# Low parts over the raw chunk, seven raw and four high-part buffers, one instruction per expert chunk and engine

## The reference, cut to what matters

```python
for l in range(2):                     # two hybrid layers: attention, convolution, spatial gate, block attention
    x = x + hybrid_layer(x, ...)       # h @ w_in [1024, 3488], then y @ w_out [1024, 1024]
h = rmsnorm(x);  x = x + hybrid_mixer(h, ...)         # w_in [1024, 2048], w_out [1024, 1024]
h = rmsnorm(x);  x = x + (silu(h @ wg) * (h @ wu)) @ wd    # dense, 2816 wide
h = rmsnorm(x);  x = x + hybrid_mixer(h, ...)
h = rmsnorm(x);  x = x + moe(h)                       # 8 experts, 3584 wide, each token goes to 2
return rmsnorm(x)
```

```python
top_v, top_i = lax.top_k(h @ w_router, 2)
gates = softmax(top_v)                                # spread over the 8 experts as gate
y = sum(gate[:, e:e+1] * ((silu(h @ wg[e]) * (h @ wu[e])) @ wd[e]) for e in range(8))
```

## Time and profile before

| | us |
|---|---|
| runs, median (lowest to highest) | 1587.7 (1586.84 to 1590.16) |
| span of the profiled execution | 1585.3 |
| TensorE busy | 1519.5 (96%) |
| VectorE busy | 1293.3 (82%) |
| ScalarE busy | 1091.0 (69%) |
| GpSimd busy | 119.5 (8%) |
| DMA, moved | 462.70 MB, mean 292 GB/s |

### The profile page before, as it was taken

One profiled execution on the slowest core, in us unless ns is written; L12 is line 12 of the kernel. 1 busy time (PEld: TensorE's weight loads), 2 busy tenths in 40 slices (PEclk: granted clock), 3 DMA queues, 4 the chain that ended last, 5 costly groups with the idle time before them and its releaser, 6 DMA issues.

```text
span 1585.3 us, 20833 instructions
## 1 busy us (share of the span) xinstructions
PE 1519.5 (96%) x7379; PEld 1259.7 (79%) x7379; DVE 1293.3 (82%) x1595; ACT 1091.0 (69%) x1435; POOL 119.5 (8%) x242
## 2 busy tenths in 40 slices
PE   7999999999999999699999999999899999999995
PEld 5788788888888888588887788888788787788784
DVE  5686585566545556789999999999999999999998
ACT  3664565655434364278888788888788878788876
POOL 3433431101000010100000000000000000000000
PEclk9999999999999999699999999999999999999998
DMA  9645444535546554299999999999999999999995
GB/s 329 208 150 177 158 151 140 186 107 186 173 146 208 191 182 138 67 323 377 391 397 407 386 369 387 386 407 407 383 386 387 391 409 400 382 386 387 398 409 221
DMA packets 203364, 462.70 MB, mean 292 GB/s; under 512 B 7934, under 2 KB 12428, under 8 KB 203132
## 3 DMA queue, kind: packets, MB, share of 16 engines
q1 hardware_dynamic: 200304, 453.80, 78.5%
q0 software_dynamic: 1904, 5.38, 1.3%
q10 hardware_dynamic: 1052, 2.19, 0.4%
HBM read 460.29 MB, written 1.05 MB: 291 GB/s over the span
## 4 chain that ended last, share of the span: by engine, by line
PE 76%; DVE 10%; DMA 7%; issue 2%; DVEq 2%; ACT 2%; SPq 0%; ACTq 0%
PE ps L2080 8%; PE ps L2082 8%; PE ps L2081 8%; PE ps L2536 8%; PE ps L2538 7%; PE ps L2537 7%; PE ps L2551 7%; PE ps L2552 7%; DVE wlo_sb L1304 5%; DMA raw_sb<-moe_wu 4%; PE ps L2589 2%; DMA raw_sb<-w_in 2%; ACT whi_sb L929 1%; DMA raw_sb<-moe_wd 1%; PE ps L2498 1%
## 5 line engine op out<-in xcount | busy, mean ns | idle before, releaser
L1304 DVE TENSOR_TENSOR wlo_sb<-raw_sb,whi_sb 128x1024 fp32r<-128x1024 f32 x672 | 783.6, 1218 | 38.1 <-ACT whi_sb L929 35.8
L929 ACT ACTIVATE whi_sb<-raw_sb 128x1024 fp32r<-128x1024 f32 x672 | 667.2, 1051 | 156.5 <-PE ps L2538 102.5
L1296 DVE TENSOR_TENSOR wlo_sb<-raw_sb,whi_sb 128x1024 fp32r<-128x1024 f32 (+2 forms) x198 | 230.2, 1204 | 143.3 <-ACT whi_sb L921 142.3
L921 ACT ACTIVATE whi_sb<-raw_sb 128x1024 fp32r<-128x1024 f32 (+2 forms) x198 | 192.3, 1023 | 161.5 <-PE ps L2082 131.1
L2080 PE MATMUL ps<-whi_sb,xlo_sb 128*128 128x512 f32 (+2 forms) x544 | 213.2, 392 | 4.2 <-DVE xlo_sb L1343 4.2
L2081 PE MATMUL ps<-wlo_sb,xhi_sb 128*128 128x512 f32 (+2 forms) x544 | 209.0, 384 | 0.0
L2082 PE MATMUL ps<-whi_sb,xhi_sb 128*128 128x512 f32 (+2 forms) x544 | 208.9, 384 | 0.0
L2536 PE MATMUL ps<-whi_sb,xlo_sb 128*128 128x512 f32 x448 | 181.3, 405 | 4.5 <-DVE wlo_sb L1304 3.8
L2538 PE MATMUL ps<-whi_sb,xhi_sb 128*128 128x512 f32 x448 | 175.4, 391 | 0.0
L2551 PE MATMUL ps<-whi_sb,xhi_sb 128*128 128x512 f32 x448 | 175.2, 391 | 0.0
L2552 PE MATMUL ps<-wlo_sb,xhi_sb 128*128 128x512 f32 x448 | 174.6, 390 | 0.0
(11 more groups left out here) (386 smaller groups left out, 2107.3 us busy)
## 6 DMA issues: line engine op xcount, KB each, us to landing
raw_sb<-moe_wg SPq DMA_DIRECT2D x115, 1024.0 KB, 9.7
raw_sb<-moe_wu SPq DMA_DIRECT2D x112, 1024.0 KB, 10.2
raw_sb<-moe_wd SPq DMA_DIRECT2D x112, 1024.0 KB, 10.8
raw_sb<-w_in SPq DMA_DIRECT2D x40, 1024.0 KB, 5.2
raw_sb<-w_out SPq DMA_DIRECT2D x16, 1024.0 KB, 5.0
raw_sb<-ffn_wg SPq DMA_DIRECT2D x10, 1024.0 KB, 5.1
raw_sb<-ffn_wu SPq DMA_DIRECT2D x10, 1024.0 KB, 5.1
raw_sb<-ffn_wd SPq DMA_DIRECT2D x10, 1024.0 KB, 5.1
```

Source lines behind the costliest of these rows:

```text
L921: nc.scalar.activation(whi[i % SPLIT][:, c:c + k // 2, 0:n], raw[i % RAW][:, c:c + k // 2, 0:n], ACT.Copy).then_inc(hi_ready, 1)
L929: nc.scalar.activation(whi[i % SPLIT][:, c:c + KC // 2, :], raw[i % RAW][:, c:c + KC // 2, :], ACT.Copy).then_inc(hi_ready, 1)
L1296: op = V.tensor_tensor(wlo[i % SPLIT][:, c:c + k // 2, 0:n], raw[i % RAW][:, c:c + k // 2, 0:n], whi[i % SPLIT][:, c:c + k // 2, 0:n], ALU ...
L1304: op = V.tensor_tensor(wlo[i % SPLIT][:, c:c + KC // 2, :], raw[i % RAW][:, c:c + KC // 2, :], whi[i % SPLIT][:, c:c + KC // 2, :], ALU.su ...
```

## The change

Three things change at once.

1. The low part of a chunk is written over its own raw buffer, so there are as many low-part buffers as raw ones and no others. The raw buffers go from six to seven, the high-part buffers from three to four; in all 11 buffers of 8 KB per partition in place of 12. SyncE now waits for `split_used` of chunk n-7 before it issues chunk n.
2. SPLIT is four: at place i, ScalarE and VectorE convert chunk i+4. A buffer's index is the chunk's number in the whole row, modulo 7 or 4.
3. For the experts' chunks ScalarE and VectorE use one instruction of 128x2048 each, and VectorE waits for the whole high part. The dense part keeps its halves.

Nothing else in the order of the work is touched. The diff, cut to its core (the matmuls take their operands from `whi_of` and `wlo_of` in the same way everywhere):

```diff
-RAW = 6
-SPLIT = 3
+RAW = 7
+SPLIT = 4
...
+        over_raw = ExitStack()
+        wlo = [sb(f"wlo{i}", [PART, KC, NC], F32R, stack=over_raw) for i in range(RAW)]
+        over_raw.close()
         raw = [sb(f"raw{i}", [PART, KC, NC]) for i in range(RAW)]
         whi = [sb(f"whi{i}", [PART, KC, NC], F32R) for i in range(SPLIT)]
-        wlo = [sb(f"wlo{i}", [PART, KC, NC], F32R) for i in range(SPLIT)]
...
+        def raw_of(c0, i):
+            return raw[(c0 + i) % RAW]
+        def whi_of(c0, i):
+            return whi[(c0 + i) % SPLIT]
+        def wlo_of(c0, i):
+            return wlo[(c0 + i) % RAW]
...
         def sp_chunk(sp, src, c0, i, chunk, per=0, l=0):
             if c0 + i >= RAW:
-                sp.wait_ge(lo_ready, number(c0, i - RAW + 1, per, l))
+                sp.wait_ge(split_used, number(c0, i - RAW + 1, per, l))
...
         def act_hi_moe(act, i, l):
-            act.wait_ge(raw_landed[i % RAW], landed(AT_MOE, i, PER, l))
+            act.wait_ge(raw_landed[(AT_MOE + i) % RAW], landed(AT_MOE, i, PER, l))
             act.wait_ge(split_used, number(AT_MOE, i - SPLIT + 1, PER, l))
-            for c in range(0, KC, KC // 2):
-                nc.scalar.activation(whi[i % SPLIT][:, c:c + KC // 2, :], raw[i % RAW][:, c:c + KC // 2, :],
-                                     ACT.Copy).then_inc(hi_ready, 1)
+            nc.scalar.activation(whi_of(AT_MOE, i)[:, :, :], raw_of(AT_MOE, i)[:, :, :], ACT.Copy).then_inc(hi_ready, 1)
...
         def dve_lo_moe(dve, i, l):
-            for c in range(0, KC, KC // 2):
-                dve.wait_ge(hi_ready, 2 * AT_MOE + 2 * i + (2 if c else 1) + 2 * PER * l)
-                op = V.tensor_tensor(wlo[i % SPLIT][:, c:c + KC // 2, :], raw[i % RAW][:, c:c + KC // 2, :],
-                                     whi[i % SPLIT][:, c:c + KC // 2, :], ALU.subtract)
-            op.then_inc(lo_ready, 1)
+            dve.wait_ge(hi_ready, 2 * (AT_MOE + SPLIT) + i - SPLIT + 1 + PER * l)
+            V.tensor_tensor(wlo_of(AT_MOE, i)[:, :, :], raw_of(AT_MOE, i)[:, :, :], whi_of(AT_MOE, i)[:, :, :],
+                            ALU.subtract).then_inc(lo_ready, 1)
```

More of the change, by code:

```diff
@@ L322, in head_scale_of @@
     return MLA_QK ** -0.5 if att < DEPTH and d < 2 else HD ** -0.5
-assert all(n % RAW == 0 for n in (len(HYBRID), AT_MIX0, AT_FFN, AT_MIX1, AT_MOE, PER))
+assert PER % RAW == 0 and PER % SPLIT == 0
 def build(nc, A):
@@ L914, in act_hi @@
             n, k = split_shape(chunks[i % len(chunks)])
-            act.wait_ge(raw_landed[i % RAW], landed(c0, i, per, l))
+            act.wait_ge(raw_landed[(c0 + i) % RAW], landed(c0, i, per, l))
             if not (isinstance(l, int) and c0 + i + per * l < SPLIT):
@@ L2079, in pe_chunk @@
                     first, last = chunk.first and c == 0, chunk.last and c == chunk.k - 1
-                    mm(out, lo, whi[i % SPLIT][:, c, 0:chunk.n], start=first, stop=False)
-                    mm(out, hi, wlo[i % SPLIT][:, c, 0:chunk.n], start=False, stop=False)
-                    op = mm(out, hi, whi[i % SPLIT][:, c, 0:chunk.n], start=False, stop=last)
+                    mm(out, lo, whi_of(c0, i)[:, c, 0:chunk.n], start=first, stop=False)
+                    mm(out, hi, wlo_of(c0, i)[:, c, 0:chunk.n], start=False, stop=False)
+                    op = mm(out, hi, whi_of(c0, i)[:, c, 0:chunk.n], start=False, stop=last)
             op.then_inc(split_used, 1)
@@ L2125, in pe_out @@
                     first, last = chunk.first and c == 0, chunk.last and c == KC - 1
-                    mm(acc[:, g, t, :], lo, whi[i % SPLIT][:, c, :], start=first, stop=False)
-                    mm(acc[:, g, t, :], hi, wlo[i % SPLIT][:, c, :], start=False, stop=False)
-                    op = mm(acc[:, g, t, :], hi, whi[i % SPLIT][:, c, :], start=False, stop=last)
+                    mm(acc[:, g, t, :], lo, whi_of(c0, i)[:, c, :], start=first, stop=False)
+                    mm(acc[:, g, t, :], hi, wlo_of(c0, i)[:, c, :], start=False, stop=False)
+                    op = mm(acc[:, g, t, :], hi, whi_of(c0, i)[:, c, :], start=False, stop=last)
             if done:
@@ L2535, in heavy_step @@
                         w = c * (chunk.n // NC) + h
-                        mm(o, lo, whi[i % SPLIT][:, w, :], start=first, stop=False)
-                        mm(o, hi, wlo[i % SPLIT][:, w, :], start=False, stop=False)
-                        op = mm(o, hi, whi[i % SPLIT][:, w, :], start=False, stop=last)
+                        mm(o, lo, whi_of(AT_MOE, i)[:, w, :], start=first, stop=False)
+                        mm(o, hi, wlo_of(AT_MOE, i)[:, w, :], start=False, stop=False)
+                        op = mm(o, hi, whi_of(AT_MOE, i)[:, w, :], start=False, stop=last)
                 op.then_inc(split_used, 1)
@@ L2550, in light_step @@
                         w = c * (chunk.n // NC) + h
-                        mm(o, both, whi[i % SPLIT][:, w, :], start=first, stop=False)
-                        op = mm(o, both, wlo[i % SPLIT][:, w, :], start=False, stop=last)
+                        mm(o, both, whi_of(AT_MOE, i)[:, w, :], start=first, stop=False)
+                        op = mm(o, both, wlo_of(AT_MOE, i)[:, w, :], start=False, stop=last)
                 op.then_inc(split_used, 1)
```

19 lines of the change are left out of this document (10 added, 9 removed).

## The result

| | before | after |
|---|---|---|
| median of the runs, us | 1588.9 (1586.8 to 1590.3) | 1642.0 (1641.2 to 1643.6) |
| ratio of the times, 95% interval | | 1.0334 (1.0321 to 1.0346) |
| span of the profiled execution, us | 1585.3 | 1639.4 |

The forecast was 1609.7 us, with a range of 1594 to 1618. The sign was right; of the 53 us it had 22.

The account below looks back on a forecast made before the run. Transfers were taken to lead the expert pairs, TensorE the dense part; 6.9 + 0.8 - 0.8 + 5.8 + 5.8 + 3.5 = 22.0 us on 1585.3 gave 1607.3, plus 2.4 for the median 1609.7 us, range 1594 to 1618.

Parts of the forecast that it names:

- (a): Start: low parts of chunks 4 and 5 move ahead of squares and angles; TensorE resumes at 48.5, not 41.6, +6.9 us.
- (b): Late up-projections: gated products wait for the next chunk's landing, leaving DMA idle at up-to-down changes, +5.8 us (0 to 7).
- the transfers lead: Expert pairs: transfers need 223.4 us of a pair's 225.1, so they set the pace; TensorE needs less per chunk there.
- (c): Turn of a pair: result reads stand behind the next conversion; +5.8 us (0 to 9) for the second and third turn.
- a rival at 0.11: Turns: longer TensorE stands bring the lower clock two or three times, +8 us, 1617.7 us; chance 0.11.
- (d): Tail: repeats the turn's delay with nothing behind to hide it, +3.5 us (2 to 4.5).
- The first turn: First turn of a pair: one more ready chunk fills a third of TensorE's 2.6 us stand, -0.8 us.
- The signs: TensorE back near 48 us, same dense length, landing after about 5 us, waits 2+ us longer, pairs 228 to 230 us.
- The cover: Tight places: transfers issued 2.9 and 1.1 us later, leaving 0.5 to 2.0 us of queue; no loss by itself.
- The merged instructions: Expert conversions: 2.29 us against 2.36 for the pair, 0.07 less; throughput gain taken as 0.
- the rival in which VectorE leads: Expert pairs: if VectorE's 216.8 of 225.1 us hold them, merging gives 24 us, 1570.6 us; chance 0.06.
- head start: Start of the expert part: up to seven chunks lie ready instead of nine, +0.8 us.

Follow-up runs that it names:

- e10: e6 with the start's squares, row scale and angles ahead of the low parts of chunks 4 and 5; 1601.8 us, ratio 1.0088.
- e6: e5 with VectorE's gating product of place i+1 also ahead of the low part of chunk i+4; 1606.5 us, ratio 1.0118.
- e5: Changed kernel with the reads of a job's result (places 80 and 83) ahead of the conversion of chunk i+4; 1619.0 us, ratio 1.0195.
- e3: Changed kernel with three high-part buffers, conversions at their old places and in halves, keeping seven raw buffers with low parts in place; 1598.1 us, ratio 1.005.
- e7: Changed kernel with conversions at their old places and in halves, keeping seven raw and four high-part buffers; 1588.8 us, ratio 0.9999.
- e2: Changed kernel with conversions at their old places (chunk i+3 at place i), merged instructions and four high-part buffers kept; 1592.6 us, ratio 1.0029.
- e1: Changed kernel with the experts' conversions in halves again, all else as changed; 1629.1 us, ratio 1.026.
- e4: Kernel before with merged expert conversions alone (six raw, three high-part, three low-part buffers, old places); 1608.9 us, ratio 1.0138.
- e9: e7 with products and results ahead of conversions, and the start's squares, row scale and angles ahead of low parts; 1599.5 us, ratio 1.008.
- e12: e7 with the start's order alone: squares and row scale ahead of the second half's low parts, angles ahead of chunk 4's; 1586.9 us, ratio 0.9992.

## Why the prediction was wrong, step by step

**The start (a) was right: 6.9 forecast, 6.0 measured.** The chain came as written down. It answers to the earlier trace rows:

```profile
34.05 2.36 DVE L1309 TENSOR_TENSOR wlo_sb<-raw_sb,whi_sb 128x1024 fp32r<-128x1024 f32 x2 [8.19 <-ACT whi_sb L936]
36.33 0.68 DVE L1361 CUSTOM_DVE_ANT_0 xs_sb<-x_sb 128x512 f32<-128x512 f32 x1
...
39.50 2.35 DVE L1309 TENSOR_TENSOR wlo_sb<-raw_sb,whi_sb 128x1024 fp32r<-128x1024 f32 x2
...
45.73 0.20 POOL L721 TENSOR_TENSOR rx_sb<-rx_sb,rs_tmp_sb 128x2 f32<-128x2 f32 x1
46.02 1.27 ACT L983 ACTIVATE P_sb<-ps,rx_sb 128x512 f32<-128x512 f32 x2 [0.20 <-POOL rx_sb L721]
```

POOL ended 6.2 us behind the squares' end (39.7), not 8.8, so TensorE resumed at 47.3 where I had 48.5. Behind it the dense part kept its length. Run e10 took the two low parts out of this chain and got 4.7 us back.

**The late up-projections (b) are the step that failed.** I priced a late product only where the queue of transfers was short, once per pair, 5.8 us in all, since "the transfers lead" and TensorE "needs less per chunk there". The wait itself was smaller than the lateness that I had, 1.1 us on average in place of 3.7, but it came at each of seven blocks in each pair: 22.9 us of waits in the three pairs (7.2, 8.4 and 7.3) against 4.9 before. And none of it was free. Two blocks of the middle pair show this by the start of their transposes, the first two lines before, the last two after:

```profile
1184.35 0.66 PE L2635 MATMUL ps<-con_sb,act_h_sb 128*128 128x128 f32 x4
...
1204.91 0.66 PE L2635 MATMUL ps<-con_sb,act_h_sb 128*128 128x128 f32 x4
```

```profile
1215.76 0.66 PE L2646 MATMUL ps<-con_sb,act_h_sb 128*128 128x128 f32 x4 [0.99 <-DVE act_h_sb L1995]
...
1237.59 0.66 PE L2646 MATMUL ps<-con_sb,act_h_sb 128*128 128x128 f32 x4 [1.14 <-DVE act_h_sb L1995]
```

A block took 20.6 us before, without a wait, and 21.8 after. From the first to the last of the pair's seven transposes it was 123.0 us before (1143.3 to 1266.3) and 128.8 after (1172.6 to 1301.4), 5.8 us more, and TensorE's waits for products in between grew by 5.4 (1.9 to 7.3). The windows of four heavy and four light up-projection chunks say the same, the first before, the second after:

```profile
1187.70:1208.30 20.60, 20.60 (x102) 17.17 (x101) 20.16 (x22) 17.99 (x23) 0.00 (x0) 1.00 1.05 387
```

```profile
1219.10:1241.00 21.90, 20.77 (x102) 17.18 (x101) 20.18 (x13) 18.02 (x15) 0.00 (x0) 1.00 1.05 387
```

Eight such chunks take the transfers 8 x 2.71 = 21.7 us and took TensorE 20.6. Before, chunks lay ready and TensorE ran a pair's first blocks at its own 20.6 us; only in the last two did it meet the transfers, and only there did it wait for products. I called these 1.1 us a block slack. After, the product of every block stands behind a conversion that waits for a landing, so TensorE goes at the pace of the transfers or below it from the first block on (21.5 to 22.5 us for the pair's first five): in the middle pair ScalarE's conversions wait for a landing 40 times, where it was 15. Nothing of this came back later: the down-projections, from the last transposes to the end of the heavy job, took 71.8 us before and 72.5 after, against 28 x 2.56 = 71.7 us of transfers. My term took the fuller of two nearly equal resources as the only one. Products first (e6 against e5) gave back 12.5 us; I had 5.8 for all of (b).

**The turn (c): 5.8 forecast for two turns, 7.8 of waits and 7.6 of lower clock measured.** TensorE's wait at the heavy job's scatter grew by 3.0 and 3.2 us at the second and third turn, where I had +3.7 for its lateness, and at the light job's by 0.8 at each (1.93 to 2.71, 2.01 to 2.78). I subtracted the queue of the transfers from it (0.9 and 0.5 us), which TensorE's own chain doesn't do. On top came what I had as a rival at 0.11, at 8 us: the lower clock, behind stands of 4.4 and 2.8 us. Four stretches of 3.4 to 5.2 us at half the clock cost half their length, and a fifth stands behind the last scatter (d): 10.1 us in all. Waits for results and clock together went away in e5: 23.0 us by the runs.

**The first turn** was forecast 0.8 us better, and TensorE's stand for the low part of a chunk there did shrink, from 2.80 to 1.67 us; but the light job's scatter behind it, which had not been waited for, now waits 2.0 us. The first pair as a whole, for which the forecast had +0.8 and this -0.8, became 5.0 us longer, with 4.3 us of waits for products.

**The tail (d): 3.5 forecast, 2.7 of waits and 2.5 of lower clock measured.** The term was for the last heavy scatter. It lies inside the last pair's window, here before and then after:

```profile
1564.27 0.50 PE L2511 MATMUL ps<-yglo_sb,backT_sb 128*128 128x512 f32 x1 [1.62 <-DVE yglo_sb L1974]
```

```profile
1616.14 0.79 PE L2522 MATMUL ps<-yglo_sb,backT_sb 128*128 128x512 f32 x1 [4.32 <-DVE yglo_sb L1985]
```

So this term was about right. What comes behind the last chunk (the window called the tail above) is 0.3 us shorter: nothing lands there any more, so nothing stands ahead of the last result.

**The signs.** Of those that I had named, TensorE's return at 48 us and the length of the dense part came. Behind a turn the time from issue to landing fell to 5.1 to 5.5 us and the transfers stopped, as said; at the up-to-down change it is 7.9 us in the middle pair, not 5, so the queue whose end (b) was priced by was not used up. The waits at the scatters grew by more than 2 us at the heavy jobs only, those at the products by 1. A pair took 237 to 239 us, not 228 to 230.

**The cover.** The later issue alone was priced at zero. Run e3 has it at 5 to 11 us with three high-part buffers, and the fourth buffer takes nearly all of it back (e7): the two almost cancel, not by the mechanism that I wrote down. With TensorE's stands the later issue does more: SyncE now waits for TensorE, so the stands at a turn stopped the transfers, which no run takes apart from the stands themselves. Writing in place costs nothing that shows: half a low part took 1221 ns in e7 and 1218 before.

**The merged instructions.** The duration was right: 2289 ns measured, 2.29 us forecast, against 2.36. VectorE's busy time fell by 3.5 us in the middle pair and bought nothing. The latency, with all that came of it, cost 3.9 us at the old places (e2 against e7), 13 at the new ones (after against e1), 21.5 with three high-part buffers (e4). The sentence of the Trainium skill (Perfetto Trace Analysis, Optimizing Scalar/DVE Operations) that speaks for splitting where these engines aren't saturated but cause bubbles held in all three, although VectorE was busy for 96% of the pairs before; its rule for grouping, the rival in which VectorE leads, held in none.

**What stays open.** The 49 us of e2 hold the old places and a spare high-part buffer at once. In halves the place without the spare buffer is about 31 us (e1 against e3) and the spare buffer 4 to 9 (e7 against e3); with merged instructions, old places with three buffers in place were not run. With the nine places and the start mended (e10, 1601.8) the changed kernel is still 9.2 us over the one at old places (e2, 1592.6). The two profiled executions differ by 10.1: 4.5 of it lie in the first pair (261.2 against 256.7), some 3 in the other pairs and 2 in the tail; which of the other 75 early conversions does it wasn't tried. Nor was it shown why a start 3.9 us sooner is given back in the first pair (e9) and not in e12, where a dense part that ends 2.0 us sooner became 1.9 us in the median against e7 (1.1 by the ratios to the kernel before), within the noise.

The sum by term, in us:

| term | forecast | measured |
|---|---|---|
| start | 6.9 | 6.0 |
| first pair (head start, first turn) | 0.0 | 5.0 |
| products, pairs 2 to 4 | 5.8 | 18.0 (waits) |
| results, second and third turn | 5.8 | 7.8 (waits) |
| light result at the first turn | 0 | 2.0 (waits) |
| last heavy result (d) | 3.5 | 2.7 (waits) |
| lower clock, pairs 2 to 4 | 0 (rival) | 10.1 (busy) |
| rest of TensorE's busy time, pairs 2 to 4 | 0 | 4.0, cause not shown |
| other waits, pairs 2 to 4 | 0 | -1.2 |
| behind the last chunk | 0 | -0.3 |
| sum | 22.0 | 54.1 |

## What to carry to other kernels

Where engines run one written order, a deeper prefetch moves every conversion ahead of the small work behind it, and once data arrives just in time that work waits for a transfer which it doesn't need: keep the number of buffers apart from the place in the order. When two resources are both nearly full (here 223.4 us of transfers and 218.4 of TensorE in a pair of 224.8), price a delay on each of them separately, and don't call the slack of one stretch spare before the whole period has been added up. And look at what a late engine stops: here a buffer that waits for TensorE's use makes its stand a stand of the transfers. An instruction merged to save a fixed cost costs its latency at every hand-over, and a lower share of busy time on its engine is no gain where the engine isn't what the end waits for.

## What the hardware showed that was not expected

The lower clock does not go by the length of the stand before it. In the kernel before, a stand of 2.80 us was followed by 6.0 us at a granted clock of 0.50, the level already in force when TensorE came back (889.7 to 895.7). In the changed kernel two stands of the same length, 4.37 and 4.36 us, were followed by 5.2 us at 0.50, in force at once, and by 3.4 us at 0.51 that began 0.9 us after TensorE had resumed; the stands of 2.7 and 2.8 us at the light jobs' scatters brought 3.4 us each. A stand of 2.20 us in e5 brought 3.4 us (1500.0 to 1503.4), and so did stands of 1.93 and 2.01 us in e3, while stands of 1.93 and 2.01 us at the same scatters in the kernel before, and one of 2.03 us after, left the clock at 1.00. So between 1.9 and 2.2 us a stand may cost nothing or 1.7 us of work, and a longer one cost 1.7 to 3.0 us whatever its length.
